# Attention of a hybrid encoder: softmax weights turned in 32x32 blocks on VectorE, products with values in eight TensorE tiles, part of the convolution gating on GpSimd

## The chip, the cores and the metric

One core of one Trainium2 chip. The metric is the device time of one launch in microseconds, the median of several runs. The engines are named TensorE (PE), VectorE (DVE), ScalarE (ACT), GpSimd (POOL) and SyncE (SP, which here only issues DMAs). Work on them is ordered by semaphores written out in the kernel; each engine takes its instructions in the order of the program.

## What is computed

Two sequences of 256 tokens pass through two layers of a bidirectional encoder of width 1024. A layer makes one input projection of its columns into windowed attention (8 query heads, 2 key/value heads, window 128, a sink logit per head) and a bidirectional Mamba-2 mixer with a width-5 depthwise convolution; then an output projection with layer norm, and a gated MLP. The parts that matter here:

```python
proj = h @ w_in
q, k, v, z, xbc, dt_raw = jnp.split(proj, splits, axis=-1)
...
m = jnp.maximum(jnp.max(sc, axis=-1, keepdims=True), sink_b)
p = jnp.exp(sc - m)
denom = jnp.sum(p, axis=-1, keepdims=True) + jnp.exp(sink_b - m)
probs = (p / denom).astype(v_blk.dtype)
return jnp.einsum("bhgqk,bkhd->bqhgd", probs, v_blk)
...
xbc = jax.nn.silu(depthwise_conv(xbc, ssd_conv_w, ssd_conv_b))
```

## The kernel before

**Units.** All weights come as units of 128x1024. A unit is loaded into a ring of five slots (`raw`), copied on ScalarE to its high part (`whi`, L622), and its low part `wlo` is either subtracted on VectorE (L1315) or, for the unit numbers in `BY_DMA` (20 to 30 before), written negated by ScalarE (L625) and completed by an accumulating DMA that GpSimd issues (L577). A projection ("G", `by_columns`, L873 to L875) is 24 matmuls of 128x512: high by high, high by low, low by high for eight column blocks, into PSUM bank `n % 2` for unit n.

**The schedule.** `mixer_schedule()` writes out one list of steps. Every engine walks the same list and takes the kinds that are its own, in that order. Step n has the projection of unit n. Units 1 to 6 are key, value and queries, 7 to 18 the twelve convolution rows (j = n - 7; 0 to 3 are B and C, 4 to 11 are x), 19 to 26 the gate z. `A0 = 8`: steps 8 to 15 carry attention group i = n - 8, a block of 128 queries t = i // 2 and half of the heads m = i % 2.

**Attention, group i.** AS: four score matmuls on TensorE (64 rows, two row tiles, L1237) into banks 2 and 3. AM: mask, row maxima and three small operations on VectorE (L1632 to L1637). AX: four exponentials with sums on ScalarE into `sc` (L803, L805); the next group's AS waits for them. AD: the denominator's reciprocal on VectorE (L1644, L1645). AN: `sc` multiplied by it on GpSimd, two halves (L583). AP, one step later: eight 128x128 transposes on TensorE into banks 4 and 5 (L1247). PT: ScalarE copies these to `p_t` (L812). AV, after every second group: eight matmuls with the values `v_tm`, 128x64, two column tiles (L1257), into an auxiliary bank; ScalarE copies the result's high part to `ahi` (L815), VectorE subtracts the low part (L1648).

**Convolution row j, in step n = j + 7.** E: ScalarE evacuates the projection with the centre tap to `cv` (L723). F, F1, F2: the four other taps on VectorE (L1478), the first two ahead of AD for i of 2 to 7 and the last two behind it. The projection of unit n waits for the taps of unit n - 2, whose bank it takes. SILU: ScalarE's tanh (L758). SIL2: VectorE's gating, (tanh + 1) times `cv` (L1485). For x rows GpSimd multiplies by D (XS, L591), and in the next step, behind the scores, TensorE transposes the row (T, L1162) and ScalarE copies it out (L776). CB: the products of C and B (L1170) in steps 12 to 15, copied out on VectorE (L1571). T, CB, AV and a few others take banks 6 and 7 in turns; `wait_aux_free` makes a use wait for the evacuation of the one two before it, by the order of the list.

**The state mixer** follows in steps 17 to 26: SB (L1196, four row tiles of 32 rows) and SF give decay logarithms, SC caps them on VectorE (L1589), SE takes exponentials on ScalarE (L789, L795), SD is the products with x (L1223, 128x64 in two column tiles).

Of the kernel before, what the change touches and what calls it, by code (L numbers as in the profile page):

```python
# [11 lines left out]

# [7 lines left out]
ALU = mybir.AluOpType  # L20
# [4 lines left out]
P = 128  # L25
DEPTH, D_MODEL, SEQ, NSEQ = 2, 1024, 256, 2
TOK = NSEQ * SEQ
# [27 lines left out]
BY_DMA = range(20, 31)  # L55
# [33 lines left out]
A0 = 8  # L89
TOP = float(np.finfo(np.float32).max)  # L90


def mixer_schedule():
    steps = []
    for n in range(U_OUT):
        i = n - A0
        steps += [("G", n), ("E", n)]
        if U_Z <= n < U_OUT - 1:
            steps += [("SW", n - U_Z)]
# [37 lines left out]
        if 0 <= i - 1 < 8:  # L137
            steps += [("AP", i - 1)]
# [21 lines left out]
        if n == 17:  # L160
            steps += [("SB", 0), ("SE", 0), ("SC", 0)]
# [50 lines left out]
def trunk(nc, x_in, units, pm_d, pf_d, cn_d, gb_d, h_d, y_d):  # L212
    ctx = ExitStack()
    with ctx:
# [51 lines left out]
        sc = [at("sc0", 34, [P, QPK, SEQ]), at("sc1", 0, [P, QPK, SEQ], start=base_h)]  # L266
        p_t = [at("p_t0", 38, [P, 2, 512]), at("p_t1", 4, [P, 2, 512], start=base_h)]
# [64 lines left out]
        y_full, xd_done, seg_full = sem("y_full"), sem("xd_done"), sem("seg_full")  # L332
# [25 lines left out]
        aux_use, y_use = {}, {}  # L358
        aux_free, y_free = [], []
        aux_counted, y_counted = {}, {}  # L360
# [8 lines left out]
        for what, i in SCHED:  # L369
            aux = lambda key, rel, c=True: take(aux_use, aux_free, aux_counted, key, rel, c)  # L370
            yy = lambda key, rel, c=True: take(y_use, y_free, y_counted, key, rel, c)
# [13 lines left out]
            elif what == "AP":  # L385
                yy(("AP", i, 0), [(pt_done, 8, i + 1)])
                yy(("AP", i, 1), [(pt_done, 8, i + 1)])
            elif what == "AV":
                aux(("AV", i), [(al_done, 4, i + 1)])
# [4 lines left out]
        AUX_N, Y_N = len(aux_counted), len(y_counted)  # L394
        def aux_bank(key):
            return 6 + aux_use[key] % 2

        def y_bank(key):
            return 4 + y_use[key] % 2
# [7 lines left out]
        def wait_y_free(eng, L, key):  # L407
            n = y_use[key] - 2
            if n >= 0:
                for s, per, count in y_free[n]:  # L410
                    eng.wait_ge(s, L * per + count)

        def wait_aux_full(eng, L, key):
            eng.wait_ge(aux_full, L * AUX_N + aux_counted[key])

        def wait_y_full(eng, L, key):
            eng.wait_ge(y_full, L * Y_N + y_counted[key])
# [1417 lines left out]
```

## Time and profile before

| what | value |
|---|---|
| median of 3 runs | 1304.26 us (1304.21 to 1304.9) |
| the profiled execution | 1304.11 us |
| its span | 1302.3 us |
| granted TensorE clock, mean | 0.998 |
| instructions | 16405 |
| busy | TensorE 1290.0, VectorE 799.6, ScalarE 604.0, GpSimd 113.7 us |

The span is the time from the first to the last recorded instruction; some 1.8 us of the device time lie around it. Busy time is that of one profiled execution, so it is compared with the span and not with the median. TensorE's matmuls overlap one another in the records: a mean of 390 ns for a matmul of 128x512 stands beside a distance of some 228 ns from start to start, so the costs of TensorE's work are read from starts.

### The profile page before, as it was taken

The page shows a single profiled execution, that of the slowest core. Times are in us where ns is not written, and L with a number is a line of the kernel's source. Part 1 is how long each engine was busy: PE and PEld are TensorE (multiplying, and loading weights), DVE is VectorE, ACT ScalarE, POOL GpSimd, SP SyncE. Part 2 cuts the span into 40 slices and gives each one's busy share as a digit, 9 for nine tenths or more (in the row PEclk, how much of TensorE's full clock was granted, in tenths as well). Part 3 has the DMA queues.
Part 4 walks back from the last instruction along what each step waited for, and adds up shares of the span by engine and source line. Part 5 has one row for each costly group of instructions (what it writes and reads, how often), then busy time and mean ns, then how long its engine had stood idle before and what let it go on. Part 6 is the DMA issues. An engine that isn't in the chain of part 4 may idle for free.

```text
span 1302.3 us, 16405 instructions
## 1 busy us (share of the span) xinstructions
PE 1290.0 (99%) x6688; PEld 1065.7 (82%) x6688; DVE 799.6 (61%) x1087; ACT 604.0 (46%) x897; POOL 113.7 (9%) x109
## 2 busy tenths in 40 slices
PE   9999999999999999999999999999999999999997
PEld 8877777889888888888898777888888888888886
DVE  7888798866444444342378987979654444443425
ACT  6765766436333333311286667653453333332112
POOL 2023511001000000000020334100000000000000
PEclk9999999999999999999999999999999999999999
DMA  5422466523333333423143216663233333334332
GB/s 200 156 65 66 97 135 132 187 64 115 98 97 97 97 97 97 129 97 98 53 137 127 65 50 141 126 187 115 80 104 95 96 98 98 98 95 128 97 97 112
DMA packets 36954, 140.77 MB, mean 108 GB/s; under 512 B 4144, under 2 KB 4560, under 8 KB 35728
## 3 DMA queue, kind: packets, MB, share of 16 engines
q1 hardware_dynamic: 33552, 127.91, 30.8%
q0 software_dynamic: 3328, 11.82, 5.4%
q8 instruction: 53, 0.87, 0.3%
q14 instruction: 21, 0.17, 0.0%
HBM read 133.42 MB, written 6.29 MB: 107 GB/s over the span
## 4 chain that ended last, share of the span: by engine, by line
PE 95%; DVE 2%; ACT 1%; issue 0%; POOL 0%; DMA 0%; DVEq 0%
PE ps L873 18%; PE ps L875 18%; PE ps L874 18%; PE ps L1010 9%; PE ps L1011 9%; PE ps L1012 9%; PE ps L899 5%; PE ps L1223 2%; PE ps L1237 1%; PE ps L1247 1%; PE ps L1257 1%; PE ps L1002 1%; PE ps L1170 1%; PE ps L1207 0%; PE ps L1196 0%
## 5 line engine op out<-in xcount | busy, mean ns | idle before, releaser
L873 PE MATMUL ps<-hhi,whi 128*128 128x512 f32 x1040 | 409.5, 394 | 0.0
L875 PE MATMUL ps<-hhi,wlo 128*128 128x512 f32 x1040 | 405.1, 390 | 0.0
L874 PE MATMUL ps<-hlo,whi 128*128 128x512 f32 x1040 | 404.8, 389 | 0.0
L622 ACT ACTIVATE whi<-raw 128x1024 fp32r<-128x1024 f32 x208 | 219.3, 1056 | 219.3 <-DMA raw<-in_units 219.3
L1315 DVE TENSOR_TENSOR wlo<-raw,whi 128x1024 fp32r<-128x1024 f32 x186 | 227.3, 1224 | 149.9 <-ACT whi L622 149.9
L873 PEld LDWEIGHTS ps<-hhi,whi 128*128 128x128 f32 x1040 | 195.2, 188 | 44.2 <-issue 4.9
L875 PEld LDWEIGHTS ps<-hhi,wlo 128*128 128x128 f32 x1040 | 195.2, 188 | 41.2
L874 PEld LDWEIGHTS ps<-hlo,whi 128*128 128x128 f32 x1040 | 195.3, 188 | 39.7
L1010 PE MATMUL ps<-whi,uhi 128*128 128x512 f32 x352 | 137.1, 390 | 0.0
L1012 PE MATMUL ps<-wlo,uhi 128*128 128x512 f32 x352 | 137.0, 389 | 0.0
L1011 PE MATMUL ps<-whi,ulo 128*128 128x512 f32 x352 | 136.9, 389 | 0.0
L1690 DVE SCALAR_TENSOR_TENSOR gcv<-ps,pf,gcv 128x510 f32<-128x510 f32 x44 | 32.9, 748 | 157.2 <-ACT gcv L843 157.2
L843 ACT ACTIVATE gcv<-ps,pf 128x512 f32<-128x512 f32 x44 | 34.3, 780 | 168.9 <-PE ps L875 162.1
L1700 DVE TENSOR_TENSOR guf<-gsg,ps 128x512 f32<-128x512 f32 x44 | 30.2, 687 | 79.0 <-PE ps L875 78.4
L1010 PEld LDWEIGHTS ps<-whi,uhi 128*128 128x128 f32 x352 | 66.1, 188 | 13.8
L1012 PEld LDWEIGHTS ps<-wlo,uhi 128*128 128x128 f32 x352 | 66.1, 188 | 13.7
L1011 PEld LDWEIGHTS ps<-whi,ulo 128*128 128x128 f32 x352 | 66.1, 188 | 13.6
L1010 PE MATMUL ps<-whi,ahi 128*128 128x512 f32 x192 | 75.8, 395 | 0.2
L1478 DVE SCALAR_TENSOR_TENSOR cv<-ps,pm,cv 128x508 f32<-128x508 f32 (+1 forms) x96 | 71.5, 745 | 7.3 <-ACT cv L723 3.0
L1011 PE MATMUL ps<-whi,alo 128*128 128x512 f32 x192 | 74.8, 389 | 0.0
L1012 PE MATMUL ps<-wlo,ahi 128*128 128x512 f32 x192 | 74.7, 389 | 0.0
L553 POOL TENSOR_TENSOR hlo<-hfm,hhi 128x512 fp32r<-128x512 f32 x16 | 21.9, 1375 | 512.8 <-ACT hhi L660 512.6
(184 smaller groups left out, 1525.1 us busy)
## 6 DMA issues: line engine op xcount, KB each, us to landing
raw<-in_units SPq DMA_DIRECT2D x208, 512.0 KB, 3.7
wlo<-in_units POOLq DMA_DIRECT2D x22, 512.0 KB, 5.7
gb<-in_gb SPq DMA_DIRECT2D x5, 1024.0 KB, 5.8
h_kept<-hb SPq DMA_DIRECT2D x2, 2048.0 KB, 9.2
ha<-h_kept SPq DMA_DIRECT2D x2, 2048.0 KB, 9.8
hb<-in_x SPq DMA_DIRECT2D x4, 512.0 KB, 5.8
out_y<-hb SPq DMA_DIRECT2D x8, 256.0 KB, 2.0
cn<-in_cn SPq DMA_DIRECT2D x1, 663.5 KB, 10.2
```

Source lines behind the costliest of these rows:

```text
L622: A(whi[:, m % RING, :], raw[:, m % RING, :], ACT.Copy).then_inc(unit_hi, 1)
L843: A(gcv[:], ps[:, bank, :], ACT.Identity, scale=pf[:, k * 3 + w0 + 1:k * 3 + w0 + 2], bias=pf[:, k + v0:k + v0 + 1]).then_inc(glu_center, 1)
L873: mm(out, whi[:, slot, cols], xhi, start=start, stop=False)
L874: mm(out, whi[:, slot, cols], xlo, start=False, stop=False)
L875: return mm(out, wlo[:, slot, cols], xhi, start=False, stop=stop)
L899: last = mm(out, w, x, start=c == 0 and kind == "hi hi", stop=stop, skip_group_check=True)
L1010: mm(ps[:, bank, :], xhi[:, rows], whi[:, slot, cols], start=start, stop=False)
L1011: mm(ps[:, bank, :], xlo[:, rows], whi[:, slot, cols], start=False, stop=False)
L1012: return mm(ps[:, bank, :], xhi[:, rows], wlo[:, slot, cols], start=False, stop=stop)
L1315: V.tensor_tensor(wlo[:, m % RING, :], raw[:, m % RING, :], f(whi[:, m % RING, :]), ALU.subtract).then_inc(unit_split, 1)
L1478: V.scalar_tensor_tensor(out=dst[:, :, lo:hi], in0=src[:, :, lo + s:hi + s], scalar=pmc("conv_w", 5 * j + tap, 5 * j + tap + 1), in1=dst[: ...
L1690: V.scalar_tensor_tensor(out=dst[:, :, 1:SEQ], in0=src[:, :, 0:SEQ - 1], scalar=pf[:, k * 3 + w0:k * 3 + w0 + 1], in1=dst[:, :, 1:SEQ], op ...
```

## The change

The eight transposes of a group on TensorE and the ScalarE copy behind them go. VectorE turns `sc` in blocks of 32x32 in one instruction (PT), in the step after the group, between AM and the first taps. What comes out has 32 keys in each group of 32 partitions, so the values are needed once for every block of 32 keys and in all four partition groups: 16 DMAs of SP's queue write them to `v_rep` behind the load of unit 12. The product of a query block becomes 64 matmuls of 32x64 weights by 128 columns (`values`), on four row tiles by two column tiles, into banks 4 to 7, and is placed after the fourth of the eight column blocks of projections 11, 13, 15 and 17. `BY_DMA` begins at 12 (eight more units a layer). The gating of rows 1 to 7 moves to GpSimd, behind a second ScalarE pass that adds the 1. SE 0 and SE 2 move behind other ScalarE work of steps 17 and 18. Buffers move: `sc1`, `p_t`, `v_rep`.

```diff
-BY_DMA = range(20, 31)
+BY_DMA = range(12, 31)
+SILU_POOL = range(1, 8)
+SQ = 32
...
+AV_AT = {A0 + 2 * t + 3: t for t in range(NBLK)}
...
+        if n in AV_AT:
+            steps += [("AV", AV_AT[n])]
         steps += [("G", n), ("E", n)]
+        if n == 18:
+            steps += [("SE", 0)]
...
-        if i in (3, 5, 7):
-            steps += [("AV", (i - 3) // 2)]
...
-        if i == 9:
-            steps += [("AV", 3)]
...
-        if 0 <= i - 1 < 8:
-            steps += [("AP", i - 1)]
...
-            steps += [("SE", 1), ("SF", 0), ("SE", 2)]
+            steps += [("SE", 1), ("SF", 0)]
...
             if not 0 <= i < 3:
                 steps += [("SIL2", n - U_CONV)]
+            if n == 18:
+                steps += [("SE", 2)]
...
-            steps += [("SB", 0), ("SE", 0), ("SC", 0)]
+            steps += [("SB", 0), ("SC", 0)]
...
             elif what == "AV":
+                aux(("AV", i, "first"), [(al_done, 4, i + 1)], False)
                 aux(("AV", i), [(al_done, 4, i + 1)])
...
+                    if n == U_CONV + RING:
+                        sp_eng.wait_ge(v_done, L + 1)
+                        sp_eng.wait_ge(own_done, L * 2 + 2)
+                        for a in range(P // SQ):
+                            for q in range(BLK // SQ):
+                                sp_eng.dma_start(v_rep[a * SQ:(a + 1) * SQ, q::BLK // SQ, :],
+                                                 v_tm[q * SQ:(q + 1) * SQ, :, :]).then_inc(v_spread, 16)
...
+                    elif what == "SIL2" and i in SILU_POOL:
+                        pool.wait_ge(conv_tanh, L * N_CONV + i + 1)
+                        pool.wait_ge(silu_done, L * N_CONV + i)
+                        x = bc[:, i, :] if i < 4 else xsc[:, i % 2, :]
+                        nc.gpsimd.tensor_tensor(x, x, cv[:, i % 2, :], ALU.mult).then_inc(silu_done, 1)
...
+                        if i in SILU_POOL:
+                            A(dst, cv[:, i % 2, :], ACT.Tanh, scale=0.5).then_inc(tanh_raw, 1)
+                            act.wait_ge(tanh_raw, L * len(SILU_POOL) + i - SILU_POOL[0] + 1)
+                            A(dst, dst, ACT.Copy, bias=1.0).then_inc(conv_tanh, 1)
...
-                        A(p_t[i % 2][:], ps[:, 4:6, :], ACT.Copy).then_inc(pt_done, 1)
...
+            def values(L, t):
+                pe.wait_ge(v_spread, (L + 1) * 256)
+                pe.wait_ge(pt_done, L * 8 + 2 * t + 2)
+                wait_aux_free(pe, L, ("AV", t, "first"))
+                wait_aux_free(pe, L, ("AV", t))
+                if t:
+                    pe.wait_ge(al_done, L * 4 + t)
+                blocks = SEQ // SQ
+                for kb in range(blocks):
+                    for a in range(P // SQ):
+                        rows = slice(a * SQ, (a + 1) * SQ)
+                        for g in range(2):
+                            last = mm(ps[g * HEAD:(g + 1) * HEAD, 4 + a, 0:QPK * SQ],
+                                      v_rep[rows, (t // 2) * blocks + kb, g * HEAD:(g + 1) * HEAD],
+                                      p_t[t % 2][rows, :, kb, 2 * g:2 * g + 2, :],
+                                      start=kb == 0, stop=kb == blocks - 1, skip_group_check=True)
+                last.then_inc(aux_full, 1)
...
+                    elif what == "PT":
+                        t, m = ATTN[i]
+                        dve.wait_ge(as_norm, 2 * (L * 8 + i) + 2)
+                        if t >= 2:
+                            wait_aux_full(dve, L, ("AV", t - 2))
+                        V.transpose(p_t[t % 2][:, m, :, :, :].rearrange("p k j q -> p j k q"),
+                                    sc[i % 2][:].rearrange("p j (k q) -> p j k q", q=SQ)).then_inc(pt_done, 1)
```

## Rows read from the trace of the kernel before

**Rows 1.** The page, part 1: busy us (share of the span) xinstructions
```profile
PE 1290.0 (99%) x6688; PEld 1065.7 (82%) x6688; DVE 799.6 (61%) x1087; ACT 604.0 (46%) x897; POOL 113.7 (9%) x109
```

**Rows 2.** Busy time by stretch: us, each engine's busy (x), PEclk, DMA share, GB/s
```profile
60.00:150.00 90.00, 90.00 (x495) 69.66 (x494) 75.58 (x133) 57.65 (x126) 30.49 (x27) 1.00 0.23 68
```

**Rows 3.** TensorE's waits: us in total, times, longest us
```profile
PE ps L1162 <- DVE xsc L1485: 2.3, 2, 1.1
```

**Rows 4.** Timeline, TensorE, 66 to 102 us: start us, us, line, out<-in, xcount
```profile
67.12 1.13 PE L1237 MATMUL ps<-qk 64*128 64x256 f32 x8
68.18 0.50 PE L873 MATMUL ps<-hhi,whi 128*128 128x512 f32 x1
68.52 0.40 PE L874 MATMUL ps<-hlo,whi 128*128 128x512 f32 x1
...
73.53 0.39 PE L875 MATMUL ps<-hhi,wlo 128*128 128x512 f32 x1
73.84 1.14 PE L1237 MATMUL ps<-qk 64*128 64x256 f32 x8
...
81.62 1.13 PE L1237 MATMUL ps<-qk 64*128 64x256 f32 x8
...
83.53 0.47 PE L873 MATMUL ps<-hhi,whi 128*128 128x512 f32 x1
...
89.19 1.13 PE L1237 MATMUL ps<-qk 64*128 64x256 f32 x8
...
92.98 0.47 PE L873 MATMUL ps<-hhi,whi 128*128 128x512 f32 x1
...
100.62 0.60 PE L1162 MATMUL ps<-cn,xsc 128*128 128x128 f32 x4
...
101.73 0.58 PE L873 MATMUL ps<-hhi,whi 128*128 128x512 f32 x1
```

**Rows 5.** Groups of instructions by shape, TensorE: busy us, mean ns | idle before
```profile
L1247 PE MATMUL ps<-cn,sc 128*128 128x128 f32 x128 | 17.8, 280 | 0.0
L1257 PE MATMUL ps<-p_t,v_tm 128*64 128x256 f32 x128 | 15.6, 385 | 0.0
```

**Rows 6.** The chain that ended last: start us, us, what
```profile
176.94 1.90 PE ps L1223 x32
```

**Rows 7.** Timeline of TensorE at 147 us
```profile
147.15 0.51 PE L1196 MATMUL ps<-heads,own_w 32*128 32x512 f32 x4
```

**Rows 8.** Groups of instructions by shape, VectorE
```profile
L1315 DVE TENSOR_TENSOR wlo<-raw,whi 128x1024 fp32r<-128x1024 f32 x186 | 227.3, 1224 | 149.9 <-ACT whi L622 149.9
...
L1571 DVE TENSOR_SCALAR cb<-ps 128x256 f32<-128x256 f32 x16 | 6.0, 414 | 0.0
```

**Rows 9.** Groups of instructions by shape, GpSimd and ScalarE
```profile
L583 POOL TENSOR_TENSOR sc<-sc,ast 128x512 f32<-128x512 f32 x32 | 32.6, 1040 | 179.3 <-DVE ast L1645 179.3
...
L625 ACT ACTIVATE wlo<-whi 128x1024 fp32r<-128x1024 f32 x22 | 23.4, 1062 | 0.7
```

**Rows 10.** Timeline of SP's queue, first 7 us
```profile
3.06 0.91 SPq L510 DMA_DIRECT2D hb<-in_x  x2
```

**Rows 11.** Timeline of VectorE, 80 to 101 us
```profile
80.66 2.38 DVE L1478 SCALAR_TENSOR_TENSOR cv<-ps,pm,cv 128x510 f32<-128x510 f32 x3
...
90.39 0.68 DVE L1632 SCALAR_TENSOR_TENSOR ps<-cn,ps 128x512 f32<-128x512 f32 x1
...
92.85 0.68 DVE L1485 SCALAR_TENSOR_TENSOR bc<-bc,cv 128x512 f32<-128x512 f32 x1
...
95.18 1.60 DVE L1478 SCALAR_TENSOR_TENSOR cv<-ps,pm,cv 128x508 f32<-128x508 f32 x2
...
96.99 1.52 DVE L1478 SCALAR_TENSOR_TENSOR cv<-ps,pm,cv 128x510 f32<-128x510 f32 x2
99.20 0.69 DVE L1485 SCALAR_TENSOR_TENSOR xsc<-xsc,cv 128x512 f32<-128x512 f32 x1 [0.70 <-ACT xsc L758]
```

**Rows 12.** Timeline of ScalarE, 80 to 101 us
```profile
87.44 1.07 ACT L622 ACTIVATE whi<-raw 128x1024 fp32r<-128x1024 f32 x1
```

More of the change, by code:

```diff
@@ L11 @@
 from contextlib import ExitStack
+import functools
 import numpy as np
@@ L265, in trunk @@
         zt = at("zt", 32, [P, TOK])
-        sc = [at("sc0", 34, [P, QPK, SEQ]), at("sc1", 0, [P, QPK, SEQ], start=base_h)]
-        p_t = [at("p_t0", 38, [P, 2, 512]), at("p_t1", 4, [P, 2, 512], start=base_h)]
+        sc = [at("sc0", 34, [P, QPK, SEQ]), at("sc1", 38, [P, QPK, SEQ])]
+        v_rep = at("v_rep", 90, [P, TOK // SQ, P])
+        p_t = [at("p_t0", 98, [P, 2, SEQ // SQ, QPK, SQ]), at("p_t1", 0, [P, 2, SEQ // SQ, QPK, SQ], start=base_h)]
         cv = at("cv", 8, [P, 2, TOK], start=base_h)
@@ L757, in _ @@
                         dst = bc[:, i, :] if i < 4 else xsc[:, i % 2, :]
-                        A(dst, cv[:, i % 2, :], ACT.Tanh, scale=0.5).then_inc(conv_tanh, 1)
+                        if i in SILU_POOL:
+                            A(dst, cv[:, i % 2, :], ACT.Tanh, scale=0.5).then_inc(tanh_raw, 1)
+                            act.wait_ge(tanh_raw, L * len(SILU_POOL) + i - SILU_POOL[0] + 1)
+                            A(dst, dst, ACT.Copy, bias=1.0).then_inc(conv_tanh, 1)
+                        else:
+                            A(dst, cv[:, i % 2, :], ACT.Tanh, scale=0.5).then_inc(conv_tanh, 1)
                     elif what == "SP":
@@ L875, in three, with by_columns @@
                 return mm(out, wlo[:, slot, cols], xhi, start=False, stop=stop)
-            def by_columns(slot, bank):
+            def by_columns(slot, bank, between=None):
                 for c in range(CT):
+                    if between and c == CT // 2:
+                        between()
                     last = three(ps[:, bank, :], slot, slice(c * P, (c + 1) * P), hhi[:, c, :], hlo[:, c, :],
@@ L1088, in _ @@
                         wait_split(pe, unit(L, i))
-                        by_columns(unit(L, i) % RING, unit_bank(i))
+                        between = functools.partial(values, L, AV_AT[i]) if i in AV_AT else None
+                        by_columns(unit(L, i) % RING, unit_bank(i), between)
                     elif what == "G":
@@ L1241, in _ @@
                         last.then_inc(as_full, 1)
-                    elif what == "AP":
-                        for kt in range(2):
-                            pe.wait_ge(as_norm, 2 * (L * 8 + i) + kt + 1)
-                            wait_y_free(pe, L, (what, i, kt))
-                            for j in range(QPK):
-                                last = nc.tensor.transpose(ps[:, y_bank((what, i, kt)), j * BLK:(j + 1) * BLK],
-                                                           sc[i % 2][:, j, kt * P:(kt + 1) * P], ident)
-                            last.then_inc(y_full, 1)
-                    elif what == "AV":
-                        pe.wait_ge(v_done, L + 1)
-                        pe.wait_ge(pt_done, L * 8 + 2 * i + 2)
-                        wait_aux_free(pe, L, (what, i))
-                        for m in range(2):
-                            for kt in range(2):
-                                for g in range(2):
-                                    last = mm(ps[g * HEAD:(g + 1) * HEAD, aux_bank((what, i)), m * 2 * BLK:(m + 1) * 2 * BLK],
-                                              v_tm[:, (i // 2) * 2 + kt, g * HEAD:(g + 1) * HEAD],
-                                              p_t[m][:, kt, g * 2 * BLK:(g + 1) * 2 * BLK],
-                                              start=(kt == 0), stop=(kt == 1), skip_group_check=True)
-                        last.then_inc(aux_full, 1)
                     elif what == "RS":
@@ L1480, in _ @@
                                                    in1=dst[:, :, lo:hi], op0=ALU.mult, op1=ALU.add).then_inc(conv_taps, 1)
-                    elif what == "SIL2":
+                    elif what == "SIL2" and i not in SILU_POOL:
                         dve.wait_ge(conv_tanh, L * N_CONV + i + 1)
+                        if i - 1 in SILU_POOL:
+                            dve.wait_ge(silu_done, L * N_CONV + i)
                         x = bc[:, i, :] if i < 4 else xsc[:, i % 2, :]
@@ L1647, in _ @@
                         dve.wait_ge(ah_done, L * 4 + i + 1)
[L1648 to L1650 removed]
+                        V.tensor_tensor(alo[:, 0:QPK, i * BLK:(i + 1) * BLK].rearrange("p j (a q) -> p a j q", q=SQ),
+                                        ps[:, 4:8, 0:QPK * SQ].rearrange("p a (j q) -> p a j q", q=SQ),
+                                        f(ahi[:, 0:QPK, i * BLK:(i + 1) * BLK]).rearrange("p j (a q) -> p a j q", q=SQ),
+                                        ALU.subtract).then_inc(al_done, 1)
+                    elif what == "PT":
[5 more added lines that the diff above has]
+                                    sc[i % 2][:].rearrange("p j (k q) -> p j k q", q=SQ)).then_inc(pt_done, 1)
                     elif what == "RP":
```

43 lines of the change are left out of this document (10 added, 33 removed).

## The prediction

> **What bounds the kernel now.** I read the page first: TensorE is busy 1290.0 us of the span of 1302.3, VectorE 61%, ScalarE 46%, GpSimd 9% [rows 1]. So the time is TensorE's work plus its idle time. The busy time by stretch says where the others have room: in the stage that the change touches in layer 0 (60 to 150 us) VectorE is busy 75.6 of 90 us [rows 2], so it is close behind. The list of TensorE's waits names only two real ones in the body of the kernel, both of 1.1 us, one per layer, for the SiLU of the last convolution row [rows 3]. Everything else arrives in time, but the view does not say by how much, and that is what the change eats into: I take it from the timelines.
>
> The sum is made against the profiled execution's 1304.1 us, 0.15 us from the median of 1304.26. A measurement of this kernel can tell about 0.2%, 2.6 us, from no change.
>
> **TensorE's work.** Removed: the transposes ("AP"). A step with scores ("AS") and transposes takes 83.53 - 81.62 = 1.91 us before the next projection starts, one with scores alone 68.18 - 67.12 = 1.06 [rows 4], so eight transposes cost 0.85 us; the first group of a layer waits a little for GpSimd and costs 0.2 more. Eight groups per layer: 7.0 us. The old product with values: scores, product and transposes take 92.98 - 89.19 = 3.79 us [rows 4], so the product costs 3.79 - 1.91 = 1.88; four per layer, 7.5 us. Their busy time in the grouped view, 17.8 and 15.6 us for both layers, agrees [rows 5]. Removed in all: 14.5 us a layer.
>
> Added: four products of 64 matmuls, each of 32x64 weights and 128 columns, on eight tiles (four row tiles, two column tiles). No row shows that tiling. Its bounds: a float32 matmul is recorded as two instructions, and the decay products (128x64, 128 columns, two column tiles) run 32 records in 1.90 us in the chain [rows 6], 0.24 us for a matmul in each tile. Four row tiles of 32 rows with 512 columns start within 0.02 us of each other (four records of 0.50 us lie in 0.51 us) [rows 7]. If both kinds of overlap combine, a product is 8 rounds of 0.22 us, 1.75 us; if only two tiles ever overlap, it is 128 records at 1.9/32, 7.6 us. I take the low end, because both neighbouring rows show full overlap in their own direction. Beside it the array changes its tiling twice in the middle of a projection: the score group costs 1.06 us for four rounds that need 0.85, and the projection after it takes 73.84 - 68.18 = 5.66 us where 24 matmuls at (73.53 - 68.52)/22 = 0.228 need 5.46 [rows 4], so about 0.4 us an insertion. That makes 2.15 us each, 8.6 a layer, and saves TensorE 5.9 us a layer.
>
> The Trainium skill (TensorE: Matmul & The Clock Gate, section "Wait — 56ns, not 53.3ns?") has a rule that speaks against this: matmul starts never come closer than about 25 ns, however few the columns; by it 128 records would be estimated at 3.2 us. The four starts within 0.02 us speak against it where tiles differ.
>
> **The other engines.** VectorE gets eight transposes of 128x1024 a layer. Nearest row: a 128x1024 operation at 1224 ns (issued every 1.13 us) [rows 8]. It reads one input where that row reads two, so half, 0.6 us, bounds it below; above I put half as much again, 1.9. I take 1.13, the row of the same size. It loses eight splits of that same size (units 12 to 19) and seven 0.69 us gatings. ScalarE loses eight copies of 128x1024, gains eight negations of 1062 ns [rows 9] and seven passes over 128x512, each as long as the tanh of that size, some 0.65. GpSimd gains seven multiplications of 1.04 us [rows 9] and eight DMA issues. As sums all of that fits, covered by a step of 9 us or so; if the cover goes it is VectorE's order that counts. The 16 small DMAs a layer sit in SP's queue ahead of the load of unit 13, which is not used until 20 us later; SP issues two in 0.91 us [rows 10], 16 take 7.5, so they cost nothing, and their data is needed some 20 us later too. The accumulating DMAs have three units of lead.
>
> **The waits that come in.** This decides it. TensorE's step gets shorter by the transposes, while the way from scores to gated row gets longer. That way, in step 11 of the schedule: masks and maxima start at 90.39 and hand over at 92.85, 2.46 us; from 95.18 to 98.51 four taps with the denominator between them, 3.33; then tanh, 0.7; the gating ends at 99.89 and the transpose that needs it starts at 100.62 [rows 4, 11]. A slack of 0.7 us. Between 92.85 and 95.18 stand a gating, the rest of the old product and a split; after the change only the block transpose, 1.13. But the gating at the end becomes tanh, a second pass on ScalarE, and 1.04 on GpSimd: 2.46 + 1.13 + 3.33 + 0.7 + 0.65 + 1.04 and 0.1 of handover, 9.4 us from the end of the scores. TensorE has there only a projection and the next scores, 5.66 + 1.06 plus 0.1 = 6.8 us, since the old product and the transposes (1.88 + 0.85 + 0.85) no longer lie between.
>
> Step by step, layer 0, from the end of the scores of the step, with the same durations:
> - Projection 11 needs the taps of 9, whose last three start at 80.66 whatever the change (they wait for the exponentials) and end at 83.04 [rows 11]. TensorE comes at 81.6: 1.4 us.
> - First product, mid-projection 11: block transpose 1 starts after the masks of step 10, about 85.45, done 86.6; TensorE comes at 86.05: 0.55.
> - Row 4's transpose in step 12: 9.4 against 6.8: 2.6.
> - Second product, in projection 13: it writes banks 4 to 7, so it waits until the other users of 6 and 7 are out, the last being the C·B copies on VectorE (two of 0.41 [rows 8]) at the end of that step: 2.46 + 1.13 + 3.33 + 0.8, and 0.25 because VectorE comes late from the step before, 7.95, against the 2.6 just lost, 1.1 for the transpose and C·B (101.73 - 100.62 [rows 4]) and 2.95 for half a projection, 6.65: 1.3.
> - Row 6's transpose: 9.4 against 1.15 + 6.8 = 7.95: 1.4.
> - Third product: 7.7 against 1.4 + 1.1 + 2.95 = 5.45: 2.2.
> - Row 8's transpose (gated on VectorE, but its tanh stands behind the exponentials, which take about 2 us and release ScalarE at 87.44 [rows 12], and behind copy, negation and evacuation, 2.65 us more): 2.46 + 2.0 + 2.65 + 0.65 + 0.7 = 8.5 against 1.15 + 5.66 = 6.8: 1.7.
> - Fourth product: no wait.
> Sum 11.15 us a layer, and I take both layers alike. The moved exponentials (SE 0 behind the evacuation of projection 18, SE 2 behind its tanh) take the old 1.1 us wait away [rows 3]. Queued behind each TensorE wait is the rest of the projection, and behind that the next scores, so none of it is made up: that engine has no spare time. Net a layer: +11.15 - 5.9 - 1.1 = +4.15; two layers: +8.3. **1304.1 + 8 = 1312 us.**
>
> **Rivals.**
> 1. *The waits do not form* (faster). The price is the stalls; the place is the six waits whose chain holds the block transpose. Break-even is 4.15/6 = 0.7 us less in each, a transpose of 0.45 us, or a gating handover that much shorter. Without any stall: 1304.1 - 2 x (5.9 + 1.1) = 1290. For it: sums of busy time all fit. Against it: the slack of 0.7 us is in the rows, and 3.6 us of cover are taken out. Halfway, 1301.
> 2. *The tiles overlap only in pairs* as in the decay products [rows 6]: 7.6 us a product, 8 x 5.85 = 47 more, 1359. For it: no row shows both directions at once. Against: each alone is full.
> 3. *The records cannot start fast enough.* The decay products start one record in 0.059 us [rows 6]; the full overlap wants one in 0.014. If half of the row's interval is the floor, a product takes 3.8 us, 8 x 2.05 = 16 more, 1328. For it: no row holds a long run that starts faster. Against: the four row tiles [rows 7]. The page's rule above, as an estimate, would make it 1324.
> 4. *VectorE's transposes are slow*, 1.9 us: 6 x 0.77 x 2 = 9 more, 1321.
>
> **Numbers.** Forecast, stalls of about this size, 1304 to 1318: 0.5. Rival 1: 0.27, most of it below 1301.7. Rival 2: 0.05. Rival 3: 0.10. Rival 4: 0.08. Range 1294 to 1328: it leaves out rival 2, half of rival 3 and the full form of rival 1, some 0.2 together. Faster by over 0.2%: 0.27; within: 0.07; slower: 0.66.
>
> **What would show it.** The list of waits for TensorE should have new entries: for the multiplication on GpSimd ahead of rows 4 and 6, for VectorE's taps ahead of projection 11, for its block transpose ahead of the first product, and for the C·B copies ahead of the second and third. Idle TensorE time should be some 20 us above the 12.3 of now, and its busy time some 12 us less. A product should lie within 1.8 us, a block transpose near 1.2 us. The wait for the SiLU of the last row should be gone. If TensorE's waits sum to under 5 us in the two stages the forecast is wrong by the stalls; if a product spans over 3 us it is wrong by the tiles.

## The result and the profile after the change

| what | before | after |
|---|---|---|
| median | 1304.24 us (1303.96 to 1304.9, 4 runs) | 1321.38 us (1320.78 to 1322.58, 4 runs) |
| ratio | | 1.0133, 95% interval 1.0121 to 1.0145 |
| the profiled execution, its span | 1304.11, 1302.3 us | 1320.78, 1319.0 us |

The change costs 17.1 us where 8 were forecast: the direction and the range held, the size did not. The page of the changed kernel, part 1, answers to [rows 1]:

```profile
PE 1283.7 (97%) x7456; PEld 1061.1 (80%) x7456; DVE 797.6 (60%) x1073; ACT 613.6 (47%) x911; POOL 143.0 (11%) x139
```

The span is TensorE's busy time and its idle time, so the 16.7 us of span split in two: busy 1283.7 - 1290.0 = -6.3, idle 35.3 - 12.3 = +23.0. The forecast had -11.8 and +20.1 (stalls of 22.3, less the 2.2 of the old wait). So by busy time 5.5 us of the miss are in TensorE's records and 2.9 in its idle time. That split is not one of causes: matmuls at a low clock that fill what would have been a wait count as busy. The stretch of [rows 2], same columns:

```profile
60.00:150.00 90.00, 77.82 (x719) 60.10 (x718) 69.77 (x119) 57.96 (x127) 37.70 (x36) 0.98 0.46 112
```

No engine is full any more: TensorE is busy 77.8 us of 90 instead of 90.0, VectorE 69.8 instead of 75.6. In such a stage the engines work in turns, and the sums of busy time no longer say what bounds. TensorE's waits, against [rows 3] (total, times, longest):

```profile
PE ps L1184 <- POOL xsc L587: 9.6, 4, 3.0
PE ps L899 <- DVE cb L1575: 5.9, 4, 2.5
PE ps L873 <- DVE cv L1480: 3.6, 4, 1.1
PE ps L899 <- issue: 3.2, 3, 1.3
PE ps L1184 <- DVE xsc L1489: 3.2, 3, 1.5
```

L1184 is the transpose of a row (T), L899 the new product, L873 a projection; L587 is GpSimd's gating. The old two waits of T11 are gone. The three new operations by shape (busy, mean ns of one; a neighbour's overlap is in the mean of L899):

```profile
L899 PE MATMUL ps<-p_t,v_rep 32*64 32x128 f32 x1024 | 17.1, 273 | 9.1 <-DVE cb L1575 5.9 <-issue 3.2
...
L1662 DVE STREAM_TRANSPOSE p_t<-sc 128x1024 f32<-128x1024 f32 x16 | 19.8, 1240 | 0.0
...
L587 POOL TENSOR_TENSOR xsc<-xsc,cv 128x512 f32<-128x512 f32 x8 | 10.2, 1269 | 6.4 <-ACT xsc L764 6.4
```

The timeline of TensorE in steps 12 and 13 shows a stall and what follows it:

```profile
99.68 1.13 PE L1259 MATMUL ps<-qk 64*128 64x256 f32 x8
103.76 0.89 PE L1184 MATMUL ps<-cn,xsc 128*128 128x128 f32 x4 [2.95 <-POOL xsc L587]
104.45 1.92 PE L1192 MATMUL ps<-bc 128*128 128x256 f32 x4
105.80 0.99 PE L873 MATMUL ps<-hhi,whi 128*128 128x512 f32 x1
...
109.30 0.40 PE L875 MATMUL ps<-hhi,wlo 128*128 128x512 f32 x1
110.13 2.08 PE L899 MATMUL ps<-p_t,v_rep 32*64 32x128 f32 x128 [0.43 <-DVE cb L1575]
```

The first twelve matmuls of projection 13 start over 109.30 - 105.80 = 3.50 us; in projection 11 the same half takes 2.63. The windows of one microsecond tell why (the eighth number is the granted clock):

```profile
104.00:105.00 1.00, 1.00 (x6) 0.91 (x5) 1.00 (x2) 0.12 (x1) 1.00 (x2) 0.52 0.00 0
105.00:106.00 1.00, 1.00 (x5) 0.82 (x3) 1.00 (x2) 1.00 (x5) 0.65 (x1) 0.50 0.00 0
106.00:107.00 1.00, 1.00 (x3) 0.73 (x3) 0.89 (x3) 1.00 (x6) 0.00 (x0) 0.50 0.60 78
107.00:108.00 1.00, 1.00 (x5) 0.80 (x4) 0.96 (x4) 0.97 (x2) 0.13 (x1) 0.77 0.96 164
```

After a wait of 2.95 us the clock is granted at 0.50, the lower of its two levels (1.2 GHz), for three microseconds. In layer 1 the same half takes 4.29 us.

In step 9 VectorE and GpSimd, after the change (L1639 and L1641 take 0.16 us where nothing holds them):

```profile
77.64 0.82 DVE L1639 SCALAR_TENSOR_TENSOR ast<-ast,pm 128x4 f32<-128x4 f32 x1
78.48 0.17 DVE L1640 TENSOR_SCALAR ast<-ast 128x4 f32<-128x4 f32 x1
78.69 0.16 DVE L1641 TENSOR_TENSOR ast<-pm,ast 128x4 f32<-128x4 f32 x1
```
```profile
77.14 1.29 POOL L587 TENSOR_TENSOR bc<-bc,cv 128x512 f32<-128x512 f32 x1 [1.51 <-ACT bc L764]
```

An operation on four columns ends at 78.46, just as GpSimd's gating does (78.43). It was held. In step 12 two of them are held one after the other, the second by GpSimd's multiplication by D, which now falls beside it:

```profile
102.94 0.79 DVE L1639 SCALAR_TENSOR_TENSOR ast<-ast,pm 128x4 f32<-128x4 f32 x1
103.96 0.88 DVE L1641 TENSOR_TENSOR ast<-pm,ast 128x4 f32<-128x4 f32 x1
```
```profile
102.44 1.26 POOL L587 TENSOR_TENSOR xsc<-xsc,cv 128x512 f32<-128x512 f32 x1 [0.71 <-ACT xsc L764]
103.79 1.04 POOL L594 TENSOR_TENSOR x_d<-xsc,pm 128x512 f32<-128x512 f32 x1
```

That is 1.35 us between the scores of step 12 and its C·B copies.

Last, the fourth product of layer 0 on TensorE's timeline:

```profile
150.70 2.05 PE L899 MATMUL ps<-p_t,v_rep 32*64 32x128 f32 x123
153.31 0.44 PE L899 MATMUL ps<-p_t,v_rep 32*64 32x128 f32 x5 [0.56 <-issue]
```

The other seven products start their 128 records within 1.81 to 1.83 us, this one within 2.78, and what it waited for is nothing that the program ordered. The granted clock is 1.00 throughout, and the extra time is one gap. The record of DMAs has a transfer of 16384 bytes for TensorE's instructions that begins at 150.94 and takes 0.92 us; the gap ends 1.4 us after it.

### The profile page after: what moved, and what is told of

Its sections match the earlier page's. It is cut to its first block, busy times and chain, and to the rows that moved or that the text cites. A ratio compares the mean times of both kernels' runs of the same rounds, so it can differ in the third digit from the quotient of the medians.

```text
span 1319.0 us, 17997 instructions
## 1 busy us (share of the span) xinstructions
PE 1283.7 (97%) x7456; PEld 1061.1 (80%) x7456; DVE 797.6 (60%) x1073; ACT 613.6 (47%) x911; POOL 143.0 (11%) x139
## 4 chain that ended last, share of the span: by engine, by line
PE 89%; DVE 6%; ACT 2%; issue 1%; DMA 0%; POOL 0%; DVEq 0%
PE ps L873 17%; PE ps L875 16%; PE ps L874 16%; PE ps L1031 9%; PE ps L1033 9%; PE ps L1032 9%; PE ps L920 5%; PE ps L1245 2%; DVE cv L1480 2%; PE ps L899 1%; DVE ast L1638 1%; PE ps L1023 1%; ACT sc L811 1%; PE ps L1259 1%; DVE ps L1636 1%
## 5 line engine op out<-in xcount | busy, mean ns | idle before, releaser
L873 PE MATMUL ps<-hhi,whi 128*128 128x512 f32 x1040 | 411.7, 396 | 3.6 <-DVE cv L1480 3.6
L1317 DVE TENSOR_TENSOR wlo<-raw,whi 128x1024 fp32r<-128x1024 f32 x170 | 207.9, 1225 | 149.4 <-ACT whi L625 149.4
L873 PEld LDWEIGHTS ps<-hhi,whi 128*128 128x128 f32 x1040 | 195.9, 188 | 51.5 <-issue 7.0
```

Of the source, the lines that this page charges most:

```text
L873: mm(out, whi[:, slot, cols], xhi, start=start, stop=False)
L1317: V.tensor_tensor(wlo[:, m % RING, :], raw[:, m % RING, :], f(whi[:, m % RING, :]), ALU.subtract).then_inc(unit_split, 1)
```

## The experiments

The theory at first: the stalls are those of the forecast, too small in size, and the long way from scores to gated row sets them. The rival: the engines work in turns, and any term taken away only shows the next wait. "The changed kernel" is the one after the change; times are medians, and before it is 1304.1 to 1304.3 in every comparison.

### One part undone or done alone

**e1, gating back on VectorE:** `SILU_POOL = range(1, 8)` becomes `range(0)`.

> The changed kernel with the gating of rows 1 to 7 back on VectorE in one instruction (no second ScalarE pass). Theory A (the loss is the longer way from scores to gated row, made longer still because GpSimd's multiplication holds up VectorE's small operations and because the 3.0 us wait ahead of row 4's transpose lets TensorE's clock fall): the wait ahead of row 4 shrinks from 3.0 to 1.0 to 1.6 us, row 6's from 1.8 to under 0.8, the granted clock stays 1.00 behind it, the small operation after the row maxima returns from 0.8 to 0.16 us, and the time is 1306 to 1312 us. Rival B (the eight-tile product and the waits for its banks are the loss): within 3 us of 1321.

Measured 1323.65 us, ratio 1.0135 to 1.0165: missed, no gain. TensorE's waits:

```profile
PE ps L899 <- DVE cb L1575: 12.2, 4, 3.4
PE ps L1184 <- DVE xsc L1489: 8.7, 8, 2.3
```

The waits for the gated row fell from 12.8 us (both entries of L1184) to 8.7, those for the bank of the C·B copies rose from 5.9 to 12.2. VectorE hands out both. The wait ahead of T4 is 2.28 us, not the 1.0 to 1.6 expected, and the granted clock still falls to 0.50 (at 102.3, for 3.4 us).

**e2, splits back on VectorE:** `BY_DMA = range(12, 31)` becomes `range(20, 31)`.

> The changed kernel with BY_DMA back at 20 to 30, so that VectorE subtracts the low parts of units 12 to 19 again. Theory A: 1.13 us more on VectorE between the masks and the taps in each step with attention, which lengthens six of the waits of each layer: 1328 to 1336 us. Rival C (the added accumulating DMAs or ScalarE's eight negations are part of the loss): the same or faster, 1312 to 1321 us.

Measured 1342.37 us (1.0277 to 1.0312), 21 slower than the change and beyond what was expected. Sixteen splits of 1.2 us cost about their whole length, as they would if VectorE's order is full. How much of it is the clock is not told apart: in this profile half projections are stretched eight times, by 10.9 us in all, and the mean granted clock is 0.984 to 0.989 in the four executions (0.994 to 0.996 for the changed kernel).

**e3, before with the gating on GpSimd alone** (the second ScalarE pass included).

> The kernel before with only the gating of rows 1 to 7 on GpSimd behind the second ScalarE pass; attention as before. Theory A: TensorE still has the transposes and the old product between, so only row 4's transpose (slack 0.7 us before) has to wait, about 1 us a layer: 1305 to 1308 us, while the small operation after the row maxima shows the 0.8 us already. Rival D (moving the gating is a loss by itself, whatever covers it): 1312 us or more.

Measured 1306.96 us (1.0011 to 1.003), as expected. The held operation is there too, a mean of 491 ns instead of 162:

```profile
L1650 DVE SCALAR_TENSOR_TENSOR ast<-ast,pm 128x4 f32<-128x4 f32 x16 | 7.9, 491 | 0.6
```

With the old product and the transposes as cover, only 2.8 us of gating and holding come through.

**e7, before with only the moves of SE 0 and SE 2:**

```diff
+        if n == 18:
+            steps += [("SE", 0)]
...
-            steps += [("SE", 1), ("SF", 0), ("SE", 2)]
+            steps += [("SE", 1), ("SF", 0)]
...
+            if n == 18:
+                steps += [("SE", 2)]
...
-            steps += [("SB", 0), ("SE", 0), ("SC", 0)]
+            steps += [("SB", 0), ("SC", 0)]
```

> The kernel before with only the two moved exponentials (SE 0 behind the evacuation of projection 18, SE 2 behind the tanh of the last row). The 1.1 us wait of each layer for the last row's gating goes: 1301.5 to 1303 us. Rival: the wait is only replaced by another one behind it, 1304.

Measured 1301.61 us (ten runs, 1301.48 to 1301.74; ratio 0.9971 to 0.999): as expected, 2.5 us under the kernel before.

### One thing moved

**e4, the product behind its projection instead of in its middle:** `between()` is called after the last column block.

> The changed kernel with the product with values behind the last column block of its projection instead of after the fourth. It comes 2.7 us later, so the waits ahead of it (1.4, 0.6, 2.6 and none, per layer) go. Theory A: the scores follow that much earlier and nothing gives it back: 1310 to 1315 us. Rival E (the wait is only moved, to the rows' transposes): 1318 to 1322 us.

Measured 1317.57 us (1.0086 to 1.0116), between the two.

```profile
PE ps L1184 <- POOL xsc L587: 10.7, 4, 3.8
...
PE ps L1184 <- DVE alo L1652: 3.0, 2, 1.5
```

The bank waits are gone, 2.6 us of projection cover them. Row transposes wait for more instead, some of it for the copies of the product itself, whose banks they take.

**e5, kept warm:** thirteen matmuls of no use into bank 4 ahead of T4 in each layer.

> The changed kernel with 13 extra 128x128 matmuls of constants (about 2.8 us, into bank 4, which nobody reads then) on TensorE between the scores of group 4 and the transpose of row 4, where it waits 3.0 us and the granted clock falls to 0.5 afterwards. Theory F (the lower clock is 1.5 us or more of the loss in each layer): the clock stays 1.00 and the time falls by 3 us, to about 1318. Rival G (the slow stretch ends in the wait for the C-B copies, which VectorE finishes at 109.87 whatever TensorE does, so the clock costs nothing): the clock stays up and the time stays within 1.5 us of 1321.

Measured 1324.92 us (1322.4 to 1326.3; 1.0136 to 1.017): no gain, and 3.5 us slower than the changed kernel, outside both expectations. Projection 13 is at full speed again (2.73 us for its first half in both layers), but the product behind it waits for the C·B copies in its turn, 9.1 us in all:

```profile
PE ps L899 <- DVE cb L1578: 9.1, 4, 2.5
PE ps L899 <- issue: 4.0, 3, 1.4
```

The second product of layer 0 starts at 109.92, 0.2 us earlier than in the changed kernel, though the half projection ahead of it took 0.8 less. So in the changed kernel the slow clock there stands in the shadow of the wait for the C·B copies. Of the products in this profile four are stretched (3.57, 2.25, 3.31 and 3.10 us), 5.0 us in all where the changed kernel loses 0.9. The windows of the four tell two kinds apart:

```profile
109.92:113.49 3.57, 2.21 (x127) 1.97 (x128) 0.00 (x0) 0.48 (x1) 2.93 (x3) 1.00 0.02 5
134.29:136.54 2.25, 2.25 (x127) 2.25 (x128) 0.00 (x0) 0.47 (x1) 1.62 (x2) 0.80 0.03 7
763.69:767.00 3.31, 3.31 (x128) 3.31 (x128) 0.00 (x0) 0.49 (x1) 2.67 (x3) 0.50 0.02 5
788.13:791.23 3.10, 3.10 (x127) 3.10 (x128) 0.00 (x0) 0.47 (x1) 2.47 (x3) 0.54 0.02 5
```

The first has one gap at full clock; the other three ran at a low granted clock. The edit did not take the low clock away, it moved it: apart from the end of the launch this profile has three stretches of 3.4 us at 0.50 (from 135.6, 763.7 and 787.6), the changed kernel two (from 104.0 and 756.0). So this run does not price a kernel whose clock stays up.

**e6, the block transpose ahead of the masks;** **e8, the same with e4's place of the product:**

```diff
+        if 1 <= i < 9:
+            steps += [("PT", i - 1)]
         if 0 <= i < 8:
             steps += [("AS", i), ("AM", i)]
```

> The changed kernel with VectorE's block transpose of group i - 1 ahead of the masks and maxima of group i and not behind them, so that it runs while VectorE waits for the scores. Theory A (TensorE and VectorE take turns: the waits hang on what VectorE does between the scores and the C-B copies): that way is 1.16 us shorter in five or six places of a layer, 1307 to 1313 us. Rival H (VectorE has no spare time there, so the place within its queue does not matter): within 3 us of 1321.

> Both edits: the block transpose ahead of the masks and the product behind its projection. Theory A: the product's waits for its banks go, and the rows' transposes wait 1.16 us less each: 1303 to 1309 us. If the two edits only take away the same wait it is no faster than the earlier block transpose alone.

Measured 1322.42 (1.0125 to 1.0155) and 1324.19 us (1.0138 to 1.0168). The theory's 1307 to 1313 and 1303 to 1309 were both missed by far; the first lies within the rival's 3 us of 1321. In e6 the exponentials have become the late ones: TensorE waits 2.0 us for them ahead of scores, which the changed kernel never does, and 10.3 instead of 9.6 for the gating; in e8 that is 2.5 and 11.9. The block transpose was ahead of the masks now, and held up the maxima that ScalarE needs.

**e9 to e12, ScalarE's copy and negation behind the tanh** instead of ahead of it; e10 with the early block transpose, e11 with the denominator behind all taps too, e12 with the gating on VectorE too.

```diff
+        if not 0 <= i < 8:
+            steps += [("SH" if n >= U_CONV else "S", n + AHEAD)]
...
             steps += [("SILU", n - U_CONV)]
+            if 0 <= i < 8:
+                steps += [("SH", n + AHEAD)]
```

> The changed kernel with ScalarE's copy and negation of the next unit (2.15 us) behind the tanh of the step's row and not ahead of it, in steps 8 to 15. Theory J (two ways of nearly equal length run side by side from the scores to the gated row: on VectorE block transpose and taps, on ScalarE exponentials, copy and negation; taking 1.2 or 2.1 us off one of them alone gives nothing): within 3 us of 1321. Rival K (ScalarE's added negations are the loss): 1312 or less.

> The earlier block transpose (which alone gave nothing) together with ScalarE's later copy and negation. Theory J: both ways are shorter, the rows' transposes wait about 0.8 us less each: 1312 to 1317 us. If each of the two was no part of the loss: 1321 as before.

> The same, and the denominators (which wait for ScalarE's exponentials) behind the last two taps. Theory J: the taps no longer wait for the exponentials, another 1 us off the way in each step, and projections 10 and 11 no longer wait for their taps: 1305 to 1312 us.

> The same, and the gating of rows 1 to 7 back on VectorE. Where VectorE has time left behind its taps the handover to a second ScalarE pass and to GpSimd (2.6 us against 0.7) is saved ahead of the rows' transposes: 1303 to 1309 us. If VectorE is full there, as in the run with only the gating moved back (1323.65), it is no faster than the one before it.

Measured 1336.15, 1334.40, 1334.11 and 1338.55 us: all four missed, 13 to 17 slower than the change. ScalarE's timeline of e9 has the reason:

```profile
85.61 1.04 ACT L628 ACTIVATE whi<-raw 128x1024 fp32r<-128x1024 f32 x1
86.68 1.06 ACT L631 ACTIVATE wlo<-whi 128x1024 fp32r<-128x1024 f32 x1
87.64 0.76 ACT L729 ACTIVATE cv<-ps,pm 128x512 f32<-128x512 f32 x1
```

The evacuation at the end starts at 87.64; in the changed kernel at 84.85. The taps behind it, and the projection that takes the bank, lose that time. I had looked at the tanh alone, not at what is queued behind the work that I moved.

### One term left out

Moving did not tell a price, so these take one term out at a time.

**e13, no gating; e14, no gating, but the same work beside the way:**

```diff
-                        nc.gpsimd.tensor_tensor(x, x, cv[:, i % 2, :], ALU.mult).then_inc(silu_done, 1)
+                        nc.gpsimd.tensor_tensor(x[:, 0:1], x[:, 0:1], cv[:, i % 2, 0:1], ALU.mult).then_inc(silu_done, 1)
+                        nc.gpsimd.tensor_tensor(zt[:], qk[:, 0, :], qk[:, 4, :], ALU.mult).then_inc(beside, 1)
```

(the last line in e14 only, with a wait of GpSimd for its own end behind it)

> The changed kernel with the gating of rows 1 to 7 left out but for one column of each row (its place in the order, its waits and its semaphore stay; the rows are not gated). It takes 1.28 us off the way to each row's transpose and gives VectorE's small operations back the 0.65 us for which they are held. Theory (the sum over the way is right, its terms were too small): T4 waits 1.1 us instead of 3.0, T6 none instead of 1.8, the later bank waits 1 us less together, projections 10 and 11 0.6 us less each, some 5 a layer: 1309 to 1313. Rival (the engines hand each other the work in turn, a term taken away only shows the next wait): 1317 or more.

> As the kernel without the gating, but GpSimd multiplies two other tiles of 128x512 into an unused one right behind it, which nobody waits for. The difference from that kernel is what GpSimd's work costs the others by being there. Theory (VectorE's small SBUF operations are held while GpSimd works, 0.65 us in each of the steps 10 to 14, on the way): 4 to 7 us above the kernel without gating. Rival (the holding falls into VectorE's spare time): within 1.5 us of it.

Measured 1317.41 us (1315.27 to 1320.54) and 1326.78 us (1323.68 to 1328.33; ratios 1.0087 to 1.0118 and 1.016 to 1.0194). The first is the rival's 1317 or more, the second 9.4 us above the first, more than the 4 to 7 expected. VectorE in step 10 of e13:

```profile
84.78 0.16 DVE L1639 SCALAR_TENSOR_TENSOR ast<-ast,pm 128x4 f32<-128x4 f32 x1
84.97 0.17 DVE L1640 TENSOR_SCALAR ast<-ast 128x4 f32<-128x4 f32 x1
```

and VectorE, then GpSimd, in e14:

```profile
85.57 0.97 DVE L1641 SCALAR_TENSOR_TENSOR ast<-ast,pm 128x4 f32<-128x4 f32 x1
86.57 0.17 DVE L1642 TENSOR_SCALAR ast<-ast 128x4 f32<-128x4 f32 x1
```
```profile
85.23 1.29 POOL L588 TENSOR_TENSOR zt<-qk 128x512 f32<-128x512 f32 x1
```

Nobody waits for that multiplication, and it delays everything: the first product starts at 88.19 instead of 86.60, T4 at 102.89 instead of 101.29, the second product at 110.47 instead of 108.06, the third at 133.24 instead of 130.10. That is 3.1 us by the third product. VectorE's operations in e14 are held by 0.80 and 0.81 us in steps 9 and 10, 1.50 in step 12, where e13 has 0.67 (the multiplication by D, which both keep, holds L1639 there), and 0.74 in step 14: 3.2 us more than in e13. So the holding is on the way, as theorised, and its size fits. The two profiled spans differ by 3.1 us too, the medians by 9.4: the profile of e13 is the slowest of its four executions, that of e14 the fastest of its own and the one with the highest granted clock (0.996 in the mean, against 0.992 to 0.994).

Taking the gating away gained less than the theory said: without it T4 comes 2.5 us earlier than in the changed kernel and the third product 2.7 us, but then that product takes 2.40 us (granted clock 0.74 in the mean) and the one after it 3.13 (one gap at full clock), and the half projection between them 3.47 instead of 2.63, at a clock granted at 0.50 in its first microsecond. At the end of projection 20 0.8 us are left of the 2.7. The bank waits stand at 10.9 us instead of 5.9. Theory and rival are each right in part: the way got shorter by its terms, and other waits and losses took most of that back.

**e15, the block transposes of groups 4 to 7 left out but for a block.**

> The changed kernel with the block transposes of groups 4 to 7 left out but for one block each (the products of query blocks 2 and 3 read old weights). 1.16 us less on VectorE in steps 13 to 16, steps before that as they are. Theory (each us of the way is a us of a wait): T6 1.1 less, the third product 1.2, T8 1.1, 3.5 a layer: 1313 to 1316. Rival: within 2 us of 1321.

Measured 1319.74 us (1.0106 to 1.0136): within the rival's 2 us. The third product starts 0.4 us earlier than in the changed kernel and the fourth 0.4. The bank wait that VectorE gave up (2.6 us instead of 5.9) is taken over by another, for ScalarE's copy of the row's transpose, 2.4 us.

**e16, one eighth of the product.**

```diff
-                for kb in range(blocks):
+                for kb in range(1):
```

> The changed kernel with only the first of the eight key blocks in the products of values: 8 matmuls instead of 64, 0.23 us instead of 1.81, so TensorE loses 1.6 us eight times, 12.7 in all. If TensorE's own work still set the time, 1308 to 1310. Theory (behind three of the four products of a layer the next scores start a way that the next transpose waits for at VectorE's pace, so shorter TensorE work comes back as waits): it gains under half, 1315 to 1320, and TensorE's idle time grows by over 6 us. A product without 128 records in a row should also lose the 0.8 us stall for instructions.

Measured 1312.83 us (1.0052 to 1.0082). It gained 8.5 of 12.9 us, two thirds, more than my theory allowed, less than a TensorE-bound kernel would. So a microsecond of the product is worth about 0.66 us here, and a microsecond of the late block transposes 0.18 (e15: 1.6 us gained for 8 x 1.16 taken away); both are means over one edit, with the gap of the fourth product and the low clock in them.

### Two at once

**e17, e1 and e4 together:** gating on VectorE, product behind its projection.

> The changed kernel with the products behind their projection and the gating back on VectorE. No small operation of VectorE is held by GpSimd's gating, no product is stretched by an instruction fetch, and the wait for the bank of the C B copies, which ate the gain of the gating alone, lies 2.6 us later. Theory (held operations and fetches are what the forecast missed): 1309 to 1314, near the 1312 forecast. Rival (VectorE's load of seven more gatings sets the pace): 1317 or more, with T or the bank waits grown by as much.

Measured 1310.75 us (1309.02 to 1311.71; ratio 1.0036 to 1.007), as expected. Alone the two moved the time by +2.3 and -3.8 us, together by -10.6. Its page and its waits:

```profile
PE 1278.3 (98%) x7456; PEld 1058.6 (81%) x7456; DVE 799.3 (61%) x1087; ACT 603.7 (46%) x897; POOL 125.1 (10%) x125
```
```profile
PE ps L1184 <- DVE xsc L1489: 7.8, 6, 2.6
PE ps L899 <- DVE cb L1575: 3.2, 4, 1.0
PE ps L1184 <- DVE alo L1652: 3.0, 2, 1.5
PE ps L873 <- DVE cv L1480: 2.6, 4, 0.7
```

Busy 1278.3 is 11.7 below before, and the forecast's term was 11.8. All eight products lie within 1.81 to 1.83 us, no projection is stretched, the granted clock is 0.999 in the mean. What is left is idle time, 28.9 us instead of 12.3. This profile is of the fastest of the four executions, 4.9 us over the kernel before; the other three have a mean granted clock of 0.995 to 0.996 and take 1.7 to 2.7 us more. The median still loses 6.5 us.

## Why the prediction was right in direction and short in size

**TensorE's work, sized right for an undisturbed array.** Rivals 2 and 3 fell: 128 records start within 1.81 us, one in 14 ns, where 1.75 was taken and 7.6 or 3.8 feared. The two overlaps multiply. From start to start the fourth product of layer 1, with nothing to wait for, and what it adds to its projection take 2.2 us, against 2.15. The busy time of e17, 11.7 us under before, agrees with the forecast's 11.8, but in part by luck: its products stand behind their projection, where nothing is inserted, which saves some 0.2 us each. The rule of the Trainium skill (TensorE: Matmul & The Clock Gate, "Wait — 56ns, not 53.3ns?") that starts come no closer than 25 ns does not hold for matmuls on different tiles.

**The step that failed: the size of the stalls, 11.15 us a layer.** The mechanism was right, and so were all the places named but one, which was not listed. Here is what TensorE loses at each place, from start to start, against the lengths that the prediction used (scores 1.06, a row's transpose and C·B 1.1, half a projection with its insertion 2.95, a whole one 5.66):

| TensorE comes to | forecast | layer 0 | layer 1 |
|---|---|---|---|
| projection 10, taps of 8 | not listed | 0.8 | 0.8 |
| projection 11, taps of 9 | 1.4 | 1.2 | 1.2 |
| first product | 0.55 | 1.4 | 1.4 |
| T4 | 2.6 | 3.0 | 3.0 |
| second product, counted from T4 | 1.3 | 2.3 | 2.3 |
| T6 | 1.4 | 1.8 | 2.1 |
| third product, counted from T6 | 2.2 | 2.7 | 2.7 |
| T8 | 1.7 | 1.6 | 1.6 |
| fourth product | none | none | none |
| sum | 11.15 | 14.7 | 15.0 |

The stalls came to 29.7 us where 22.3 were forecast, 7.4 more. With the gap of 0.96 us in the fourth product of layer 0 that is 8.4, as much as the span was off (16.7 against 8.3); the small errors in TensorE's own work cancel. The origins:
- VectorE's operations with two small SBUF inputs are held while GpSimd multiplies: 0.66 us each in steps 9 and 10, 1.35 in step 12, 0.60 in step 14 of layer 0, 3.3 in all. This is the largest term, and the prediction had it at nothing: it costed the gating on GpSimd by its own length and asked only whether GpSimd had room, not whom it disturbs. It explains the late first product (87.99, in e13 86.60, with VectorE behind by 2 x 0.66) and most of the second product's 1.0 too much, and e14 against e13 prices it at 3.1 us by the third product. The Trainium skill has the rule (SBUF — State Buffer, "SBUF: two separate sides"): GpSimd's operations and VectorE's with two SBUF inputs take one pair of ports in turn, for the whole instruction. The trace agrees: L1639, with two such inputs, ends with the gating; L1640, with one, keeps its mean of 170 ns.
- GpSimd's gating takes 1.26 to 1.29 us where 1.04 was taken from the row of AN [rows 9], whose second input is a broadcast. That lengthens the way to T4 and T6. That the broadcast makes the difference was not tried.
- The late projection 10 has nothing to do with the gating: e13 waits the same 0.69 us there. The taps of 8 end at 75.6 us in the kernel before and 75.7 in the changed one; the transposes of the first group, 1.06 us with their wait, had covered them, and the prediction began its list one projection later.

**The clock, which was no term of the sum.** After T4's 3 us wait the half projection takes 0.87 us more in layer 0 and 1.66 in layer 1, and T4 with its C·B group takes 2.04 us in layer 0, 1.20 in layer 1. That is 3.4 us of TensorE's busy time, more than half of what keeps it 5.5 us above the forecast; the rest was not taken apart. It cost next to no time: from T4 to the second product it is 6.37 us in both layers, though the half projections differ by 0.8, and 6.36 in both layers of e5 at full clock, because the product waits for the C·B copies either way. So the wait of 0.5 us that the list shows there is not the forecast's 1.3; in e5, without the slow half, it is 2.1. A slow clock and a wait for another engine are the same time counted once. In other variants the low clock falls where nothing hides it, in a product for instance.

**Two kinds of stretched product.** Over the fifteen profiles with whole products, 27 of 120 are stretched, by 0.4 to 3.9 us, and a product is easily put down to the wrong kind. In 19 the records come evenly but far apart, at a mean granted clock of 0.50 to 0.80: that is the clock. In 8 the clock is 1.00 and there is one gap of 0.83 to 3.83 us. All 8 contain the start of a 16 KB transfer of TensorE's instructions, and the gap ends 1.2 to 1.6 us after that transfer's end; 21 of the 93 unstretched ones contain such a start too, and 17 of the 19 at low clock, which stays unexplained. Seven of the 8 are the fourth product of layer 0: in the twelve profiles with the product in mid-projection it is stretched in the seven in which a fetch begins inside it and in none of the other five. Of the 24 products behind their projection none is stretched. A product is 128 matmuls and 128 weight loads; in the Trainium skill (Runtime: NRT & Kernel Launch, "Instruction fetch mechanics") 16 KiB are 256 instructions, so by that page a product uses up one such block in 1.8 us, an estimate. The same section holds that fetches hide behind the issue rate; in these 8 products that does not seem so. That the fetch is the cause is argued from these coincidences, and why the place matters was not tried.

**Block transpose, small terms.** 1.24 us each, issued every 1.16 (1.13 taken): rival 4 fell. The SE moves gained 2.5 us by themselves (e7), 2.2 forecast. The 16 small DMAs cost nothing that shows.

**Rival 1, that no waits form,** fell with the list of waits. Its reasoning about break-even does not hold either: e13 took 1.28 us and more out of the way, e15 1.16 in four places of a layer, more than the 0.7 named, and they gained 4 and 1.6 us, where the kernel before is 17 away. In this stage the price of a term is not its length times the number of waits.

**What stays open.** Why one execution of e13 or e14 differs from another by up to 5 us, beyond the granted clock; what decides whether a wait lowers the clock; whether fetches make the gaps; and whether an order of steps exists in which the block transposes pay. None of the 15 variants of the changed kernel beat the kernel before. The fastest kernel of the study that computes everything is e7, the old kernel with the moved exponentials.

## What to carry to other kernels

Work taken off the bounding engine was also the cover of every chain beside it; compute the chain's slack before the sum, and start at the first step that loses cover. A long wait can bring the engine back at half clock; whether that costs time depends on the next wait. Where a stage has gone over to turns, single edits tell nothing (+2.3 and -3.8 us alone were -10.6 together): leave terms out, or change two at once. Work given to GpSimd has two prices, its own length and what it holds up on VectorE; the second is seen in VectorE's smallest operations. Before a longer matmul sequence is explained, read the granted clock inside it.

## What the runs showed of the hardware that was not expected

- Eight tiles of 32x64 run fully in parallel: 128 matmul records start within 1.81 us, the time of eight rounds of 0.226.
- VectorE's 128x4 operation with two SBUF inputs takes 0.16 us alone and 0.82 to 0.97 while a GpSimd multiplication of 128x512 runs, ending together with it.
- The granted clock is 0.50 for some three microseconds after a 2.95 us wait of TensorE ahead of T4. The length of that wait alone does not decide it: in e1 2.28 us ahead of T4 were followed by a low stretch, in e17 2.55 were not.
- A run of 256 short instructions on TensorE lost 0.96 to 3.9 us in one gap at full clock in 8 of 120 cases, each beside a 16 KB instruction transfer of 0.9 to 1.2 us.
- A block transpose of 128x1024 float32 on VectorE takes 1.24 us, as long as an elementwise operation of that size.
